# One-core two-block network: the first projection begun by halves of the inner index, zeros between the setup's sums, gate sums one step later

## The reference

```python
ada = silu(c) @ w_ada[l] + b_ada[l]                  # 6*1024 columns
sh1, sc1, g1, sh2, sc2, g2 = split(ada, 6)
h = x * (1.0 + sc1) + sh1                            # columns 0:1024 and 1024:2048 of ada
qa, ka, va, qb, kb, vb = split(h @ w_in_ab, ...)     # 1024 x 3072 weights
y = concat(differential_attention(qa, ka, va), dilated_attention(qb, kb, vb)) @ w_o
x = layer_norm(alpha * x + (1.0 + g1) * y)           # g1: columns 2048:3072 of ada
h = x * (1.0 + sc2) + sh2;  x = layer_norm(alpha * x + (1.0 + g2) * swiglu(h))
```

## Time and profile before

| | us |
|---|---|
| median of 3 runs | 1677.32 |
| lowest, highest | 1677.19, 1680.98 |
| profiled execution | 1675.25 |
| its span in the trace | 1673.4 |
| PE busy | 1613.1 (96%) |
| DVE busy | 1086.2 (65%) |
| ACT busy | 804.9 (48%) |
| POOL busy | 224.4 (13%) |

### The profile page before, as it was taken

How to read it: one execution, slowest core, us unless ns; L and a number is a source line. 1 busy time by engine, 2 the same in 40 slices (tenths; PEclk the granted TensorE clock), 3 DMA queues, 4 the chain that set the end, 5 groups by cost and what they waited for, 6 DMA issues and landing times.

```text
span 1673.4 us, 24653 instructions
## 1 busy us (share of the span) xinstructions
PE 1613.1 (96%) x9268; PEld 1346.8 (80%) x9268; DVE 1086.2 (65%) x1332; ACT 804.9 (48%) x1033; POOL 224.4 (13%) x300
## 2 busy tenths in 40 slices
PE   3999999999999999999999999999999999999999
PEld 2997788778887888778888978888888889878887
DVE  7798877877759456765546886554555546765544
ACT  1565533336555444554346756444454345664443
POOL 2101001000000000078926200000000002200000
PEclk9999999999999999999999999999999999999999
DMA  9976787884644755465554425656466555445652
GB/s 321 334 252 203 280 293 278 280 297 127 218 148 148 271 197 178 148 190 186 189 176 151 153 89 173 199 177 198 153 202 197 179 196 161 138 160 178 198 178 99
DMA packets 225750, 330.10 MB, mean 197 GB/s; under 512 B 10423, under 2 KB 187160, under 8 KB 225678
## 3 DMA queue, kind: packets, MB, share of 16 engines
q1 hardware_dynamic: 210480, 276.93, 50.7%
q0 software_dynamic: 14800, 52.06, 9.0%
q10 hardware_dynamic: 398, 0.11, 0.0%
HBM read 327.97 MB, written 1.09 MB: 197 GB/s over the span
## 4 chain that ended last, share of the span: by engine, by line
PE 75%; DVE 12%; DMA 7%; ACT 3%; issue 2%; SPq 0%; POOLq 0%; DVEq 0%; POOL 0%; ACTq 0%
PE bank L2797 35%; PE bank L2539 22%; PE bank L2527 7%; DMA s_late<-in_w_ada 5%; DVE s_late L1924 4%; PE bank L2497 3%; DVE s_wL L1899 2%; PE bank L2809 1%; DMA s_mix<-in_w_ada 1%; PE bank L2509 1%; ACT s_wH L1459 1%; DVE s_late L1936 1%; DMA s_raw<-in_w_ffn_in 1%; PE bank L2638 1%; PE bank L2594 1%
## 5 line engine op out<-in xcount | busy, mean ns | idle before, releaser
L1899 DVE TENSOR_TENSOR s_wL<-s_raw,s_wH 128x2048 fp32r<-128x2048 f32 x251 | 581.2, 2316 | 292.2 <-ACT s_wH L1459 291.8
L1459 ACT ACTIVATE s_wH<-s_raw 128x2048 fp32r<-128x2048 f32 x254 | 485.3, 1911 | 232.0 <-PE bank L2797 139.9
L2797 PE MATMUL bank<-s_wH,s_hH 128*128 128x512 f32 x1056 | 420.9, 399 | 5.8 <-DVE s_hL L2261 3.3
L2797 PE MATMUL bank<-s_wH,s_hL 128*128 128x512 f32 x1056 | 412.6, 391 | 0.0
L2797 PE MATMUL bank<-s_wL,s_hH 128*128 128x512 f32 x1056 | 412.0, 390 | 0.0
L2797 PEld LDWEIGHTS bank<-s_wH,s_hH 128*128 128x128 f32 x1056 | 198.7, 188 | 50.6 <-issue 9.1
L2797 PEld LDWEIGHTS bank<-s_wH,s_hL 128*128 128x128 f32 x1056 | 198.5, 188 | 42.7
L2797 PEld LDWEIGHTS bank<-s_wL,s_hH 128*128 128x128 f32 x1056 | 199.0, 188 | 39.8 <-issue 0.7
L2539 PE MATMUL bank<-s_wH,s_aH 128*128 128x512 f32 x496 | 195.0, 393 | 1.1 <-DVE s_hL L2028 0.9
L2539 PE MATMUL bank<-s_wH,s_aL 128*128 128x512 f32 x496 | 193.9, 391 | 0.0
L2539 PE MATMUL bank<-s_wL,s_aH 128*128 128x512 f32 x496 | 193.7, 390 | 0.0
(11 more groups left out here) (454 smaller groups left out, 2249.3 us busy)
## 6 DMA issues: line engine op xcount, KB each, us to landing
s_raw<-in_w_ffn_in SPq DMA_DIRECT2D x88, 512.0 KB, 4.9
s_raw<-in_ffn_w_gate SPq DMA_DIRECT2D x88, 512.0 KB, 3.9
s_raw<-in_ffn_w_up SPq DMA_DIRECT2D x88, 512.0 KB, 4.9
s_raw<-in_ffn_w_down SPq DMA_DIRECT2D x88, 512.0 KB, 4.2
s_late<-in_w_ada POOLq DMA_DIRECT2D x20, 2048.0 KB, 10.3
s_raw<-in_w_ffn_out SPq DMA_DIRECT2D x44, 512.0 KB, 4.9
s_raw<-in_w_in_ab SPq DMA_DIRECT2D x24, 512.0 KB, 9.3
s_raw<-in_w_in_cd SPq DMA_DIRECT2D x24, 512.0 KB, 4.7
```

What stands on the lines that cost most here:

```text
L1459: A(wH[:, slot, :], raw[:, slot, :], ACT.Copy).then_inc(hi_ready, 1)
L1899: TTn(wL[:, slot, :], raw[:, slot, :], wH[:, slot, :].bitcast(F32), ALU.subtract).then_inc(lo_ready, 1)
L2797: last = mm(bank[GU_BANK[tt]][:], h, w[:, k, :], start=(half == 0 and k == 0 and i == 0), stop=(half == 1 and k == 3 and i == 2), skip_gro ...
```

## The change

**Setup.** The inner index is split in two halves: the first half of h (columns 0 to 511) needs only the first half of the shift and of the scale. The second piece that is loaded is therefore now the scale's first half (FIRST_COLS), x comes in two halves, and units 0 and 1 are loaded, split and multiplied by halves of their inner index: their first halves (`half_unit(u, 0)`, 24 matmuls each, 48 in all) come before the third piece's sum, their second halves after the fourth's. Between the third and the fourth piece's sums PE gets 24 matmuls of zeros, and 10 before the second halves. The fourth piece is loaded into slot 0 of `ada_raw`, where the first one was, after DVE has finished that one. DVE does the first half of h before toep and the third piece.

**Gate sums.** The first gate piece's terms move from steps 1 and 2 to 2 and 3, the following ones so that all is again at the old place from step 7 on; PE sums the first in step 4 rather than 3.

```diff
-                      (mix[:, 0:2048], mix[:, 2048:4096]), (t32[:].rearrange("p k t -> p (k t)"), mix[:, 4096:6144]))]
+                      (mix[:, 0:2048], mix[:, 2048:4096]), (ada_raw[:, 0, 0:2048], ada_raw[:, 0, 2048:4096]))]
+        FIRST_COLS = (0, 2, 1, 3)
...
-        LEAD, STEPS = 36, 13
+        EARLY = 2
+        LEAD, STEPS = (36, 36), 13
...
-        ADA_STEPS = ({1: [(1, 2, 0, 4)], 2: [(1, 2, 4, 8)], 3: [(0, 2, 0, 3)], 4: [(0, 2, 3, 6)], 5: [(0, 2, 6, 8), (1, 3, 0, 1)],
-                      6: [(1, 3, 1, 5)], 7: [(1, 3, 5, 8)], 8: [(0, 3, 0, 3)], 9: [(0, 3, 3, 6)], 10: [(0, 3, 6, 8)],
+        ADA_STEPS = ({2: [(1, 2, 0, 4)], 3: [(1, 2, 4, 8)], 4: [(0, 2, 0, 4)], 5: [(0, 2, 4, 8)],
+                      6: [(1, 3, 0, 5)], 7: [(1, 3, 5, 8)], 8: [(0, 3, 0, 3)], 9: [(0, 3, 3, 6)], 10: [(0, 3, 6, 8)],
...
-        ADA_TURN = ({3: (1, 2), 6: (0, 2), 8: (1, 3), 11: (0, 3), 13: (1, 4)}, {5: (0, 6), 9: (0, 7)})
-        ADA_DONE = ({4: (1, 2), 7: (0, 2), 9: (1, 3), 12: (0, 3), 13: (1, 4)}, {6: (0, 6), 10: (0, 7)})
+        ADA_TURN = ({4: (1, 2), 6: (0, 2), 8: (1, 3), 11: (0, 3), 13: (1, 4)}, {5: (0, 6), 9: (0, 7)})
+        ADA_DONE = ({5: (1, 2), 7: (0, 2), 9: (1, 3), 12: (0, 3), 13: (1, 4)}, {6: (0, 6), 10: (0, 7)})
...
-            sp.dma_start(x[:], a["x"][0].rearrange("(a p) d -> p a d", p=P)).then_inc(ev("x_in"), 16)
+            sp.dma_start(x[:, :, 0:512], x_in[:, :, 0:512]).then_inc(ev("x_in0"), 16)
+            half_unit(0, 0, ab_units[0])
+            half_unit(1, 0, ab_units[1])
             first_ada(2)
+            sp.dma_start(x[:, :, 512:D], x_in[:, :, 512:D]).then_inc(ev("x_in1"), 16)
+            sp.wait_ge(ada_step[0], 8)
             first_ada(3)
-            qkv("ab", a["w_in_ab"][0])
+            sp.wait_ge(ev("first_hi"), EARLY)
+            for u in range(EARLY):
+                half_unit(u, 1, ab_units[u])
+            straight("ab", ab_units, EARLY)
...
+            pool.wait_ge(ev("ada_in31"), 16)
             pool.dma_start(bias[:, 0:12, :], toep_tile(0, 12)).then_inc(toep_in, 16)
...
+            def modulated(half):
+                r, g = TR["ab"], 2 * half
+                dve.wait_ge(ada_out[0], half + 2)
+                dve.wait_ge(ada_out[1], half + 2)
+                sc = adaC[:, 0, 8 + 4 * half:12 + 4 * half]
+                step(TS(sc, sc, 1.0, None, ALU.add))
+                dve.sem_inc(ev("scale_ready"), 1)
+                dve.wait_ge(tr_done, TRD["ab"] + g + 1)
+                for c in (2 * g, 2 * g + 1):
+                    last = TS(t32[:, c, :], bank[TURN_BANK["ab"][g]][:, (c % 2) * T:(c % 2) * T + T], adaC[:, 0, 8 + c:9 + c],
+                              adaC[:, 0, c:c + 1], ALU.mult, ALU.add)
+                last.then_inc(t32_ready, 1)
+                if half == 0:
+                    split_half(0, 0)
+                lower_part(r, g)
+                lower_part(r, g + 1)
+                split_half(1, half)
...
+                if l == 0:
+                    for u in range(2):
+                        half_unit(u, 0)
+                    turn_columns(1)
+                    ada(0, 0, 1, False)
+                    pe.wait_ge(ev("toep_rows"), 1)
+                    keep_busy(1, 24)
+                    ada(0, 1, 1, False)
+                    pe.wait_ge(ev("lam_part"), 3)
+                    mm(bank[1][:, 384:385], ones[0:1, :], lam[0:1, 5:6], start=True, stop=True).then_inc(ev("lam_part"), 1)
+                    pe.wait_ge(ada_out[0], 3)
+                    keep_busy(0, 10)
+                    half_unit(0, 1)
+                    half_unit(1, 1)
+                else:
+                    dense(0, 16)
...
-                dense(16, LEAD)
+                dense(16 if l else 32, LEAD[l])
```

More of the change, by code:

```diff
@@ L1195, in qkv, with straight @@
                                  col_unit(w, m * 1536 + j * 256 + 512 * u))
-            def straight(name, units):
-                for u, src in enumerate(units):
+            def straight(name, units, first=0):
+                for u, src in enumerate(units[first:], first):
                     n = START[name] + u
@@ L1462, in split_py, with split_half @@
                 split(n % RING, n, n // RING + 1)
+            def split_half(u, half):
+                at = slice(UNIT // 2 * half, UNIT // 2 * half + UNIT // 2)
+                act_e.wait_ge(raw_full[u], 16 * half + 16)
+                A(wH[:, u, at], raw[:, u, at], ACT.Copy).then_inc(hi_ready if half else ev("first_hi"), 1)
             def ada_evac(slot, cnt, gdst=None, cdst=None, b=None):
@@ L1514, in pair_direct, with transposed @@
                 return A(blocks(hH[:, c, :]), backwards(bank[b][:, 0:T]), ACT.Copy)
-            def transposed(name, scale=None, offset=0.0, groups=4, direct=False):
-                for g in range(groups):
+            def transposed(name, scale=None, offset=0.0, groups=4, direct=False, first=0):
+                for g in range(first, groups):
                     if not direct:
@@ L1916, in ada @@
                 acc = ada_acc[:, slot, :]
[L1917 removed]
+                rows_b = ada_b[:, slot, :] if first is None else first_b[:, FIRST_COLS[first], :]
                 for k in range(KC):
@@ L2596, in turn_tile, with turn_columns @@
                         last.then_inc(tr_done, 1)
+            def turn_columns(half):
+                pe.wait_ge(ev(f"x_in{half}"), 16)
+                for tt in range(TT):
+                    for k in range(KC // 2 * half, KC // 2 * half + KC // 2):
+                        at = (k % 2) * T + tt * P
+                        last = pe.transpose(bank[TURN_BANK["ab"][k // 2]][:, at:at + P], x[:, tt, k * P:k * P + P], ident[:])
+                        if tt and k % 2:
+                            last.then_inc(tr_done, 1)
             def transposed(name):
                 busy = BUSY[name] if name in BUSY else (0, 0)
-                if name in ("ab", "cd"):
+                if name == "cd":
                     keep_busy(TURN_BANK[name][0], busy[0])
@@ L2733, in ada_turn, with half_unit @@
                     ada(l, slot, cnt, slot == 0, b)
-                dense(0, 16)
+                def half_unit(u, half):
+                    if half:
+                        pe.wait_ge(lo_ready, u + (LO0 + 1))
+                    else:
+                        pe.wait_ge(ev("first_lo"), u + 1)
+                    H, L = (w[:, u, :].rearrange("p (k c) -> p k c", k=KC) for w in (wH, wL))
+                    for pair in (2 * half, 2 * half + 1):
+                        if u == 0:
+                            pe.wait_ge(tl_ready, 4 * TR["ab"] + pair + 1)
+                        for ft in range(2):
+                            for k in (2 * pair, 2 * pair + 1):
+                                wh, wl = H[:, k, ft * P:ft * P + P], L[:, k, ft * P:ft * P + P]
+                                for i, (w, h) in enumerate(((wh, hH), (wh, hL), (wl, hH))):
+                                    last = mm(bank[4 + u][:, ft * T:ft * T + T], w, h[:, k, :], start=(ft == 0 and k == 0 and i == 0),
+                                              stop=(k == KC - 1 and i == 2), skip_group_check=True)
+                    if half:
+                        last.then_inc(unit_used, 1)
+                if l == 0:
[12 more added lines that the diff above has]
+                    half_unit(1, 1)
+                else:
+                    dense(0, 16)
                 if l == 1:
```

65 lines of the change are left out of this document (34 added, 31 removed).

## The result

The change made the kernel slower: the median of 18 runs is 1685.28 us (1677.60 to 1687.13) against 1677.26 (1674.89 to 1680.98) for the kernel before in the same job, a ratio of 1.0044 with a 95% interval of 1.0037 to 1.0052, or some 8 us. The profiled execution took 1683.99, its span is 1682.1. The forecast, 1678.7 and at most 1682.0, was wrong in size.

A forecast was written before the change was run, and what follows sets the result against it. PE, busy 96% of the span, was taken as the bound; its 3.3 us lead shrank to a 0.2 gain at pair 1's turn, and the gate tables made the net +1.4: median 1678.7 us, range 1673.7 to 1682.0.

The forecast's parts named there:

- The setup: Start of the kernel: second halves at 48.2, pair 0's scores at 55.5 in place of 58.77.
- The price of the zeros' clock: Zeros around the fourth piece's sums: nothing if the clock stays up, 11.3 us if all run twice as long; nothing taken.
- the second rival: Setup zeros run at half clock: 1684.3 if all 24 do, 1680.0 if some 3 us do; chance 0.13.
- The lead: At pair 0's scores PE is 3.3 us ahead, kept only if the partners come sooner too.
- the sum: The prediction's main account, setup to step 10: net +1.4 us, median 1678.7; chance 0.50.
- the wait of 3.9 us: Before pair 1's turn: PE arrives early and stands still for 3.9 us; turn at 79.7, gain 0.2.
- nothing behind it takes this back: From the step-10 maxima at 115.30 on, the chain goes through DVE and ACT, so the +1.4 us stays.
- The tables: Gate tables, steps 4 to 10: four more DVE terms ahead of norm 3; turn 3 +1.2 us, +1.4 by step 10.
- Load sooner: Rival before pair 1's turn: unit 6's load comes 4 us sooner, PE keeps its lead, 1674.3; chance 0.19.
- The late third gate load: Rival before norm 3: load lands 94.6 to 97.3, wanted about 95.9; up to 1680.4; chance 0.12.
- the rivals: Unit 6's load sooner 0.19, zeros at half clock 0.13, third gate load late 0.12, change does nothing 0.06.

The follow-up runs named there:

- e7: Changed kernel without the 24 matmuls of zeros between the third and fourth piece's sums: 1676.71 us, ratio to the kernel before 0.9995.
- e14: Changed kernel with 108 tiny matmuls added at PE's idle start: 1679.84 us, ratio to the kernel before 1.0020.
- e12: e7 with 24 tiny matmuls added at PE's idle start: 1684.33 us, ratio to the kernel before 1.0042.
- e1: Kernel before with the changed gate tables alone: 1677.63 us, ratio to the kernel before 1.0006.
- e17: e7 with the old gate tables: 1675.86 us, ratio to the kernel before 0.9988.
- e4: Changed kernel with the second gate load held until unit 6's load has landed: 1681.50 us, ratio to the kernel before 1.0020.
- e9: Kernel before with 34 tiny matmuls added at PE's idle start: 1681.18 us, ratio to the kernel before 1.0019.
- e6: Kernel before with 22 zeros in place of 5 in PE's wait near 375 us: 1678.36 us, ratio to the kernel before 1.0000.
- e10: Kernel before with 128 tiny matmuls added at PE's idle start: 1678.27 us, ratio to the kernel before 1.0009.
- e16: Kernel before with 108 tiny matmuls added at PE's idle start: 1676.80 us, ratio to the kernel before 1.0004.
- e13: e3 with 78 tiny matmuls added at PE's idle start: 1679.82 us, ratio to the kernel before 1.0022.
- e3: Changed kernel with 16 matmuls of zeros in PE's wait ahead of pair 1's turn: 1680.67 us, ratio to the kernel before 1.0021.
- e8: Kernel before with the change's 24 and 10 zeros alone, at their places: 1687.19 us, ratio to the kernel before 1.0052.

## Why the prediction failed

**The setup was right.** Second halves at 48.73 (48.2 forecast), a lead of nearly 3 us at pair 0's scores (56.09 against 58.77, 55.5 forecast), the zeros covered and at full clock, the sums of the fourth piece in 1.05. The eight transposes ahead of them took 1.03 us, where eight at 21.05 take 1.97. The early products ended at 36.56 and not near 34, since the first ones took 0.64 us a half step against 0.36 later; nothing waited for them. The price of the zeros' clock was rightly taken as nothing, and the second rival, half clock in the setup, did not happen in this kernel.

**The lead was lost where the sum lost it.** Unit 6 was copied at 74.89 (74.0), PE waited 3.80 (3.9) and turned pair 1 at 80.31 (79.7).

**First failed step: the wait of 3.9 us was priced at nothing but itself.** The sum let PE stand still and go on at full speed. The chain shows 6.01 for 36 matmuls, 1.5 us lost; and the earlier trace rows had shown such a thing, half clock behind an idle PE, which the text used for the setup alone. Turn 3 came at 105.13 instead of 103.4 and the step-10 maxima at +2.95 instead of +1.4. Half clock is not all of it: in e7 the clock is full there, pair 1 turns at the same 80.31, and PE still waits for DVE's norm and turns pair 3 at 104.28 (timeline of e7):

```profile
104.28 0.55 PE L2707 MATMUL bank<-s_ident,s_mix 128*128 128x128 f32 x3 [0.65 <-DVE s_mix L2057]
```

So some 0.9 us of the 1.7 by which turn 3 missed are DVE's part and the later turn 1. By the medians of e7 and e14 the 24 zeros, their position aside, cost 3.1 us in the end; the two traces show 1.6 (spans of 1675.1 and 1676.7), and where the rest is made is not shown.

**Second failed step, and the larger: "nothing behind it takes this back", and nothing behind it would add.** The feed-forward took back more than 1 us (+2.95 at 118, +1.73 at 318), and code that nobody had edited added 7. The sum knew instructions by what they do and not by where they lie. A zero matmul has a third price beside its time and its clock: 128 bytes of code (an estimate: 16 KB for 256 instructions, and two of them) ahead of 1600 us of tightly fitted work. By the pairs e7 and e12 and the changed kernel and e14, the unlucky position cost 5.4 to 7.6 us of the 8. In the two traces about 4 us come near 446 (the load 1.0, and from the turn on +4.51 grows to +7.6 by 461, at half clock), and 1.4 from the stall in the second block (the burst takes 1.75 before and 3.18 after). The 1.6 at 334 belong to neither: kernels that are not slow have that half clock too.

The Trainium skill, "Runtime: NRT & Kernel Launch", section "Instruction fetch mechanics", says that code is refilled in blocks of 256 instructions and that crossing a border is mostly hidden. The traces agree with the count; with "mostly hidden" they disagree here: a stall of about 1 us at a border in a burst, and 24 tiny matmuls for 7.6 us.

**The tables** were priced at 1.2 by turn 3, and in e1 turn 3 came 1.25 us later (103.26 against 102.01 in the timelines). In the median they cost 0.6 alone and 0.85 between e7 and e17, neither to be told from nothing.

**The rivals.** "Load sooner" was shown wrong, and e4 shows why it mattered less than thought: even with the gate load held, unit 6 comes only 2 us sooner. The late third gate load did not decide: DVE waits for no load between 86 and 106. None of the rivals was the true one.

**What stays open.** That code position decides is shown, by e7 and e12, e9, and e14. How it makes the gate load later is not. A packet of code beside it is one reading, but packets inside the load did no harm in e6 (at 438.1, 1.3 us before its end; the load took 8.89) and in e14 (at 442.6, 1.1 before its end; 8.99). The time of the load goes rather with how much of SP's next unit moves beside it: 0.38 MB in 8.69 us in e7, 0.44 in 9.02 in the kernel before, 0.49 in 8.99 in e14, 0.77 in 9.95 in e9, 0.83 in 10.02 in the changed kernel. Yet SP issues these loads at the same distance from POOL's in fast and slow kernels (5.0 us ahead in the kernel before, in the changed one and in e14), so why they overlap more is not known. Nor is it settled when the clock falls. It falls behind a wait of 1.72 us at 330 in the changed kernel and not behind one of 1.68 in the kernel before, and e1, e7, e10 and e16 show the same fall there without being slow; it falls behind 1.47 us at 445 in e6 and not behind 1.71 at 454 in e13. The length of the wait alone does not decide it.

## What to carry to other kernels

Filler matmuls can keep a clock up (1.00 in e3 where the changed kernel has 0.50), though they did not in e8, and they are code: price them by what stands behind them in the program too, and before believing a difference of half a per cent, shift the code by some harmless instructions and measure again. A lead that the next partner doesn't share turns into waiting, and a wait of several microseconds can be paid twice, once as itself and once by the slower work behind it: 1.5 us behind the wait of 3.80 here, some 3 behind that of 2.60.

## What the runs showed of the hardware

The DMA view has packets of 16 KB on a queue "instruction", one for about 256 instructions of PE. In a burst of small matmuls PE stalls for about 1 us (0.92 to 1.60 over all runs) at a place that moves with the number of matmuls ahead and comes back after 128 of them, 256 instructions. Where these borders lie moved whole kernels by 4.4 to 7.6 us of 1680 in three comparisons (e9, the changed kernel and e14, e7 and e12) and by 1.5 us or less in two (e10, e16), against the 1.4 us that was forecast for the change.
